# Part of the attention layer's input work placed among the expert layer's last picks, and table pieces placed in a down projection

## What is computed

```python
# expert layer: for each token 8 heads x 16 picks; u and v rows are gathered
act = gelu(einsum('pd,phkd->phk', xb, u_tab[idx]));  coef = gate * act
y = einsum('phk,phkd->pd', coef, v_tab[idx])
# attention layer: h = rmsnorm(x, norm1_g) * (1 + scale) + shift, for context and x
p = h @ w_in;  q = p[..., :1024];  k = rmsnorm(p[..., 1024:1280], kn_g);  v = p[..., 1280:1536]
q_l = apply_rope(rmsnorm(q_l, qn_g), cos, sin);  k_l = apply_rope(k_l, cos, sin)
# attends from x alone, to keys and values of context and x; then @ w_out
# feed-forward: h = x @ w_up (5632 wide); convolution over 3 tokens; (silu(g) * up) @ w_down
# S5: a diagonal complex recurrence; its powers come from tables of 32 x 256 complex numbers per row
```

## Time and profile before

| | us |
|---|---|
| median of 3 runs | 4437.26 (4435.03 to 4441.18) |
| the profiled execution | 4438.26 |
| its span, first to last instruction | 4436.5 |
| PE busy | 3674.1 (83%) |
| DVE busy | 2562.2 (58%) |
| peer_a's picks, first dot to last sum | about 1244 to 2589 |
| POOL's issue of one gather, 768 of them | median 0.946, at most 1.994 |
| Attention | about 2592 to 2741 |
| Ffn 0: first product, down projection, end | 3631, 3810, 3888 |

### The profile page before, as it was taken

How to read it: one execution, slowest core, us unless ns; L and a number is a source line. 1 busy time by engine, 2 the same in 40 slices (tenths; PEclk the granted TensorE clock), 3 DMA queues, 4 the chain that set the end, 5 groups by cost and what they waited for, 6 DMA issues and landing times.

```text
span 4436.5 us, 59216 instructions
## 1 busy us (share of the span) xinstructions
PE 3674.1 (83%) x22791; PEld 1989.2 (45%) x22791; DVE 2562.2 (58%) x5863; ACT 969.1 (22%) x2601; POOL 1257.3 (28%) x1273
## 2 busy tenths in 40 slices
PE   6898899888989987777777788887777889865999
PEld 2457744576444432222222235543222468432684
DVE  1345634556366777776777655667776349367341
ACT  0233312332132222222222213222222120010100
POOL 1005300242024444443444400344443000036000
PEclk7798899889999999999999999999999989976999
DMA  9410012000289999999999943999999324320443
GB/s 378 161 50 4 3 57 76 31 4 3 95 327 398 418 416 419 417 415 408 410 415 414 414 152 101 396 417 419 411 414 415 112 83 137 124 71 10 137 152 123
DMA packets 269478, 1043.49 MB, mean 235 GB/s; under 512 B 19394, under 2 KB 103596, under 8 KB 170896
## 3 DMA queue, kind: packets, MB, share of 16 engines
q0 software_dynamic: 114736, 815.52, 45.2%
q1 hardware_dynamic: 154464, 224.18, 15.0%
HBM read 1038.55 MB, written 1.08 MB: 234 GB/s over the span
## 4 chain that ended last, share of the span: by engine, by line
PE 49%; DMA 27%; DVE 13%; ACT 4%; POOL 4%; issue 4%; DVEq 0%; POOLq 0%; ACTq 0%
DMA arena<-in_peer_uv,arena 25%; PE psum L261 13%; PE psum L1748 10%; PE psum L299 4%; PE psum L742 4%; PE psum L1706 4%; PE psum L781 2%; DVE arena L1883 2%; DMA arena<-in_ada_w 2%; PE psum L212 2%; PE psum L1174 1%; POOL arena L2933 1%; POOL arena L1841 1%; PE psum L1083 1%; PE psum L1094 1%
## 5 line engine op out<-in xcount | busy, mean ns | idle before, releaser
L1748 PE MATMUL psum<-arena 128*128 128x512 f32 x3072 | 1454.9, 618 | 399.7 <-ACT arena L1783 393.8
L1883 DVE SCALAR_TENSOR_TENSOR arena<-arena 128x1024 bf16<-128x1024 f32 x768 | 940.9, 1225 | 526.2 <-DMA arena<-in_peer_uv,arena 493.4
L1841 POOL DMA_INDIRECT arena<-in_peer_uv,arena x768 | 863.4, 1124 | 1181.9 <-PE psum L1748 1036.5
L1748 PEld LDWEIGHTS psum<-arena 128*128 128x128 f32 x3072 | 571.9, 195 | 1234.2 <-ACT arena L1783 643.9
L261 PE MATMUL psum<-ring,arena 128*128 128x512 f32 (+2 forms) x1408 | 589.2, 581 | 25.5 <-DVE arena L2762 9.1
L261 PEld LDWEIGHTS psum<-ring,arena 128*128 128x128 f32 x1408 | 266.8, 197 | 342.1 <-issue 315.1
L1776 ACT ACTIVATE arena<-arena 128x2 f32<-128x2 f32 x384 | 78.2, 204 | 1248.7 <-DVE arena L1883 1248.7
L1783 ACT ACTIVATE arena<-consts,arena 128x128 f32<-128x128 f32 x768 | 268.4, 394 | 224.4 <-DVE arena L1895 220.9
L299 PE MATMUL psum<-arena,ring 128*128 128x256 f32 x1408 | 308.3, 380 | 9.2 <-DVE arena L2757 7.7
L299 PEld LDWEIGHTS psum<-arena,ring 128*128 128x128 f32 x1408 | 266.0, 190 | 49.5 <-issue 7.2
L742 PE MATMUL psum<-arena,ring 128*128 128x512 f32 x512 | 229.7, 603 | 1.6 <-issue 1.6
(11 more groups left out here) (401 smaller groups left out, 4000.7 us busy)
## 6 DMA issues: line engine op xcount, KB each, us to landing
arena<-in_ada_w SPq DMA_DIRECT2D x48, 1024.0 KB, 14.5
ring<-in_ffn_w_up SPq DMA_DIRECT2D x44, 1024.0 KB
ring<-in_dn_w_in SPq DMA_DIRECT2D x24, 1024.0 KB
ring<-in_peer_w_query SPq DMA_DIRECT2D x22, 1024.0 KB
ring<-in_ffn_w_down SPq DMA_DIRECT2D x20, 1024.0 KB
arena<-in_peer_uv,arena POOLq DMA_INDIRECT x768, 12.9
ring<-in_ev_w_in SPq DMA_DIRECT2D x10, 1024.0 KB
ring<-in_dn_w_out SPq DMA_DIRECT2D x8, 1024.0 KB
```

Source lines behind the costliest of these rows:

```text
L1748: m = e.matmul(k.banks[4 + t % 2 * 2 + nh], self.diag[g % self.ND], self.vsl[g % self.NS][:, nh * 512:(nh + 1) * 512], start=u % 8 == 0 an ...
L1841: e.indirect_dma_start(self.uv[g % self.NS], None, self.table(), bass.IndirectOffsetOnAxis(ap=self.eid[u % 6][:, s:s + 1], axis=0)).then_i ...
L1883: e.scalar_tensor_tensor(self.junk[g % 2], self.us[g % self.NS], 1.0, self.h[:, u // 8, :], MUL, MUL, accum_out=self.a[u % 2][:, s:s + 1]) ...
```

## The change

It has two parts.

**Norm, keys and values of attention.** A new class `EarlyRows` puts the norm of tiles 0 to 2 and their key and value projections into units 27 to 31 of peer_a, one step behind a pick s of unit u, with number i = 16 (u - 27) + s. ACT takes three squares (i = 0, 2, 4), one root with a table load (i = 8), six groups of four modulations (i = 22 to 40) and two pairs of copies (i = 52, 68). DVE takes a mean, a reciprocal and three scalings (i = 6, 11, 12, 14, 27). PE takes 8 transposes at each of i = 17, 21 and 33, and two products of 128x512 at i = 29 and then at every fourth step from 37 to 77. Attention keeps the norm of tile 3 and its 8 products; then come the queries. SP loads the key and value blocks ahead of the query blocks. DVE now works on the keys first and normalises the queries behind the last copy of the projection; the keys' transposes stand on PE ahead of the queries' ones.

**Table pieces.** In Ffn 0, DVE takes two pieces behind each convolution for c = 3 to 11 as before, and one from c = 12 on. What is left, 24 pieces, comes behind the last convolution, ahead of the additions of the down projection.

```diff
+    def early(self, u, s):
+        return 16 * (u - 27) + s if self.nt > 2 and u >= 27 else None
@@ Peer.pe_sum, and in the same way Peer.act and Peer.dve
+            if self.early(u, s) is not None:
+                k.early.pe(e, self.early(u, s))
@@ EarlyRows
+    def act(self, e, peer, i):
+        if i in (0, 2, 4):
+            e.activation(self.sq, st.k.X[:, t, :], ACT.Square, ..., accum_out=self.var[:, t:t + 1])
+        elif i == 8:
+            e.activation(self.var, self.var, ACT.Sqrt, bias=0.0, scale=1.0).then_inc(*S.up("n_sd"))
+        elif i in (22, 24, 26, 28, 38, 40):
...
+        elif i in (52, 68):
+            self.put(e, {52: 0, 68: 1}[i])
+    def pe(self, e, i):
+        if i in (17, 21, 33):
...
+        elif i >= 29 and i % 4 == 1:
+            n = 0 if i == 29 else (i - 33) // 4
+            if n < 12:
+                self.pe_kv(e, n // 4, n % 4 * 2, 2)
@@ Attention.sp
-        for p in (self.qp, self.kvp, self.op):
+        for p in (self.kvp, self.qp, self.op):
@@ Attention.pe
-        self.norm.pe(e)
-        for mark in self.norm.marks():
-            e.wait_ge(*mark)
+        e.wait_ge(*V.at("l_x"))
+        for half in range(2):
...
+        self.early.pe_kv(e, 3, 0, 8)
         self.qp.pe(e)
+        e.wait_ge(*S.at(("v", 3)))
+        for t in range(4):
+            self.kt[t].pe(e)
         e.wait_ge(*V.at(("q", 1, 512)))
-        self.kvp.pe(e)
-        e.wait_ge(*S.at(("v", 3)))
         self.qt.pe(e)
@@ Ffn
     def pieces(self, c):
-        return 0 if self.l or c < 3 else 2
+        return 0 if self.l or c < 3 else 2 if c < 12 else 1
@@ Ffn.dve
+        for _ in steps:
+            pass
         for n0 in (0, 512):
```

More of the change, by code:

```diff
@@ L1869, in dve @@
                     self.dve_coef(e, u, s // 2)
+                if self.early(u, s) is not None:
+                    k.early.dve(e, self.early(u, s))
             for _ in steps:
@@ L2060, in dve, with __init__, bank, put @@
                 e.tensor_scalar(dst, st.k.banks[4 + n % 4][:, 0:dst.shape[1]], self.sm[:, n:n + 1], None, MUL).then_inc(*V.up(("put", n)))
+class EarlyRows:
+    def __init__(self, st, kvp, A, B):
+        self.st, self.kvp, self.A, self.B = st, kvp, A, B
+        a = st.k.arena
+        self.sq, self.xn, self.var = a[:, 4096:5120], [a[:, 5120:6144], a[:, 6144:7168]], a[:, 12000:12003]
+    def bank(self, t):
+        return self.st.k.banks[(4, 5, 4, 5)[t]]
+    def act(self, e, peer, i):
+        st, P, V, S = self.st, self.st.P, self.st.V, self.st.S
+        if i in (0, 2, 4):
+            t = i // 2
+            e.wait_ge(*peer.V.at(("x", t)))
+            if t:
+                e.wait_ge(*S.at(("n_sq", t - 1)))
+            e.activation(self.sq, st.k.X[:, t, :], ACT.Square, bias=0.0, scale=1.0,
+                         accum_out=self.var[:, t:t + 1]).then_inc(*S.up(("n_sq", t)))
+        elif i == 8:
+            e.wait_ge(*V.at("n_mean"))
+            e.activation(self.var, self.var, ACT.Sqrt, bias=0.0, scale=1.0).then_inc(*S.up("n_sd"))
+        elif i in (22, 24, 26, 28, 38, 40):
+            t, half = {22: (0, 0), 24: (0, 1), 26: (1, 0), 28: (1, 1), 38: (2, 0), 40: (2, 1)}[i]
+            e.wait_ge(*P.at(("nt", t, half)))
+            for c in range(4 * half, 4 * half + 4):
+                e.activation(st.hT[:, c, t * 128:(t + 1) * 128], self.turned(t, half)[:, c % 4 * 128:(c % 4 + 1) * 128],
+                             ACT.Identity, scale=self.A[t][:, c:c + 1], bias=self.B[t][:, c:c + 1]).then_inc(*S.up(("nT", t, half)))
+        elif i in (52, 68):
+            self.put(e, {52: 0, 68: 1}[i])
+    def put(self, e, t):
+        st, S = self.st, self.st.S
+        e.wait_ge(*st.P.at(("kv", t)))
+        e.activation(st.kk[:, t, :], self.bank(t)[:, 0:256], ACT.Copy, bias=0.0, scale=1.0).then_inc(*S.up(("k", t)))
+        e.activation(st.v[:, t, :], self.bank(t)[:, 256:512], ACT.Copy, bias=0.0, scale=1.0).then_inc(*S.up(("v", t)))
+    def dve(self, e, i):
+        st, P, V, S = self.st, self.st.P, self.st.V, self.st.S
+        if i == 6:
+            e.wait_ge(*S.at(("n_sq", 2)))
+            e.tensor_scalar(self.var, self.var, 1.0 / 1024, 1e-06, MUL, ADD).then_inc(*V.up("n_mean"))
+        elif i == 11:
+            e.wait_ge(*S.at("n_sd"))
+            e.reciprocal(self.var, self.var).then_inc(*V.up("n_rs"))
+        elif i in (12, 14, 27):
+            t = {12: 0, 14: 1, 27: 2}[i]
+            e.wait_ge(*V.at("n_rs"))
+            if t == 2:
+                e.wait_ge(*P.at(("nt", 0, 1)))
+            e.tensor_scalar(self.xn[t % 2], st.k.X[:, t, :], self.var[:, t:t + 1], None, MUL).then_inc(*V.up(("n_x", t)))
+    def turned(self, t, half):
+        return self.st.k.banks[2 * t % 4 + half]
+    def pe(self, e, i):
+        st, P, V, S = self.st, self.st.P, self.st.V, self.st.S
+        if i in (17, 21, 33):
+            t = {17: 0, 21: 1, 33: 2}[i]
+            e.wait_ge(*V.at(("n_x", t)))
+            if t == 2:
+                e.wait_ge(*S.at(("nT", 0, 1)))
+            for half in range(2):
+                for c in range(4):
+                    m = st.turn(e, self.turned(t, half)[:, c * 128:(c + 1) * 128],
+                                self.xn[t % 2][:, (half * 4 + c) * 128:(half * 4 + c + 1) * 128])
+                m.then_inc(*P.up(("nt", t, half)))
+        elif i >= 29 and i % 4 == 1:
+            n = 0 if i == 29 else (i - 33) // 4
+            if n < 12:
+                self.pe_kv(e, n // 4, n % 4 * 2, 2)
+    def pe_kv(self, e, t, k0, nk):
+        st, P, V, S, ring = self.st, self.st.P, self.st.V, self.st.S, self.st.k.ring
+        if k0 == 0:
+            if t < 3:
+                e.wait_ge(*S.at(("nT", t, 1)))
+            if t == 2:
+                e.wait_ge(*S.at(("v", 0)))
+            if t == 3:
+                e.wait_ge(*S.at(("v", 1)))
+        for q in range(k0, k0 + nk):
+            key = (st.name, "kv", 0, q // 4 * 4)
+            if q % 4 == 0:
+                e.wait_ge(*ring.ready(key))
+            w = ring.buf(key).rearrange("p (k n) -> p k n", k=4)
+            m = e.matmul(self.bank(t), st.hT[:, q, t * 128:(t + 1) * 128], w[:, q % 4, :], start=q == 0, stop=q == 7)
+            if t == 3 and q == 3:
+                m.then_inc(*P.up())
+                ring.free(key, P)
+        if k0 + nk == 8:
+            m.then_inc(*P.up(("kv", t)))
+            if t == 3:
+                ring.free(key, P)
@@ L2069, in __init__ @@
         A, B = k.mod_cols(1, 0, range(4))
-        self.norm = Norm(self, range(4), self.hT, A, B, scr)
+        self.A, self.B, self.scr = A[3], B[3], scr
         self.q, self.kk, self.v = k.al2(2, 1024), k.al2(4, 256), k.al2(4, 256)
```

72 lines of the change are left out of this document (48 added, 24 removed).

## The result

| | before | changed |
|---|---|---|
| median of the runs, us | 4436.15 (4433.40 to 4441.18, 4 runs) | 4410.60 (4407.88 to 4411.86, 4 runs) |
| profiled execution, us (its span) | 4438.26 (4436.5) | 4411.86 (4410.1) |

The account below looks back on a forecast made before the run. Gathers were taken to bound the picks, a chain nearly all on PE attention, DVE Ffn 0's convolutions. 1.0 - 11.4 - 15.5 = -25.9 us from 4438.3 gave 4412.4, forecast as 4412 us, range 4403 to 4425.

Parts of the forecast that it names:

- What bounds the picks: Units 27 to 31 of peer_a: gathers at DMA share 1.01 are the bound, so work put there costs nothing if slots refill.
- The term of +1.0 us: Picks of units 27 to 31: the added work lengthens them by 1.0 us in sum.
- its 0.5 for the lumps: Picks: added work on PE, ACT and DVE, between nothing and the lumps at full length, taken as 0.5 us.
- its 0.45 for the two last products: End of unit 31: two products behind pick 13 are not covered and delay the last pair by 0.45 us.
- The port: Picks: DVE's three scalings might hold up POOL's gather issues, at worst 2.3 us in all; nothing was taken.
- Attention: From tile 3's addition to the first scores: 67.2 us in place of 78.6, 11.4 us less.
- the clock: Attention's eight key products: PE at its lower clock level costs 0 to 3.5 us; 1.0 was taken.
- Part 2: Ffn 0, c = 12 to 43: one piece per tile leaves PE the bound, 107.06 us for 122.55, 15.5 less.
- (a): Rival, units 27 to 31: ACT or PE delays are not caught up; 4424 us, to 4436; chance 0.14.
- (b): Rival, picks: slot loop without slack, every lump delays the gathers, 44 us in all; 4456 us; chance 0.04.
- (c): Rival, Ffn 0: something that remains holds PE or DVE, only half comes back; 4420 us; chance 0.12 together with (d).
- (d): Rival, attention: PE stays at its lower clock through the scores longer, rounds lose up to 5; 4417; 0.12 with (c).

Follow-up runs that it names:

- The second part alone: The kernel before with one table piece from c = 12 on and the rest in the down projection; median 4419.42 us, ratio 0.9950.
- the first alone: The changed kernel with two table pieces behind each convolution as before, norm, keys and values still among the picks; median 4430.24 us, ratio 0.9979.

## Why the prediction was right, step by step

- **What bounds the picks.** Right. The gathers run at 1.01 of the DMA engines with 6.7 us more of PE's work in the window, and the stretch from unit 27's first dot to the last pick product is as long as before. The term of +1.0 us was too large, by 1.1: of its 0.5 for the lumps nothing came that stands out of the scatter, and its 0.45 for the two last products shrank to 0.16 (6.07 us from the last dot to the last product for 5.91), since the last pair, which starts 5.25 us behind the one before it in place of 4.98, then takes 3.60 us without a gap ahead of it, and not 3.70.
- **The port.** The prediction took nothing for it, with up to 2.3 us at worst. Nothing is what came, -0.1 us over 80 picks with three scalings of 0.75 us on DVE among the gathers. The Trainium skill's page "SBUF — State Buffer", section "Who interferes with whom", has POOL's descriptors wait for such a scaling. The trace agrees for two of the three, each of which held one issue of a gather (the rows under the experiments), for 0.15 and 0.28 us; the third met none. The 1.93 us of the earlier trace rows were not a scaling's doing but a dot's, which ran from 2339.23 to 2340.45. The dots do this to some 200 issues in each trace, with the gathers at 1.0 of the DMA engines, so the slots hid such waits long before the scalings came.
- **Attention.** 67.9 us for 67.2, 10.7 less than before and not 11.4. Its terms, from the chain above: norm of tile 3 7.28 (7.2 forecast), key products 8.97 to the start of the queries' (6.9 + 1.0), queries 27.67 (27.7), copies 2.05 (2.4), queries' norm 19.17 (19.2), transposes and the last copy 2.75 (2.8). The step that was mis-sized is the clock: it cost 2.0 us, inside the 0 to 3.5 given, where 1.0 was taken. The bound itself was added up wrongly: seven products of 0.87 us at half speed would cost 6.1 us more, not 3.5. The kernel with added products showed that it is the clock (7.10 us at 1.00); over the other executions without such products the eight took 8.61 to 10.07 us, so the cost is 1.5 to 3.0 us, and 2.0 is one draw of it. The rest is the copies', 0.35 less.
- **Part 2.** 107.05 us for 107.06 forecast. The late pieces had 6.4 us of cover left, 10 forecast: they took 30.0 us for 29, and the first sum came 2.3 us earlier. The 2.3 us at the down projection's start were missing from the sum: the earlier trace rows gave the 38.72 us that DVE waits there, but I did not ask at what clock PE starts behind the gap that the late convolutions leave. The second part alone has all of this gain (38.47 us), the first alone 0.6 of it (40.18 for 40.75); why the first has any stays open.
- **The sum.** -0.1 - 10.7 - 15.5 - 2.3 = -28.6 against -25.9 worked out; 1.1 of the difference is the picks, 2.3 the clock of the down projection, less 0.7 in attention. The profiled execution came to 26.4 less only because the unchanged stretches add 2.2. So the nearness of 4410.6 to 4412 is in part luck: the terms were short of the gain by 2.7 us, and scatter of nearly that size stood against it.
- **The rivals.** (a) falls by the picks' stretch, (b) by the executions with more lumps on ACT and PE. The windows' free time on PE, 10 us per 41, was the right measure for (b)'s point of decision, and the reading that three engines' lumps add up was not: with 44 products more, where PE alone is over, the changed kernel's gain is gone. (c) falls, the pace is PE's throughout. (d), a cold array for longer at the scores, falls: the rounds and the output took 70.27 us as before. There was something to be had there all the same, 1.45 us, since before they had begun cold too.

## What to carry to other kernels

Where a stretch is bound by transfers with several buffers ahead, work for the other engines is free there up to the idle time of the fullest engine, summed over the stretch and not lump by lump (shown here for PE, with lumps of 1.7 to 3.5 us, and for ACT with lumps of 2.8 us, where the limit was not reached); add it up for the engine that gets the most, since beyond it every us counts. Where work is moved out of a chain, look for what it covered: here 19 us of a norm on DVE stood bare behind it, and splitting it, so that half runs beside the projection, brought 7.8 us more. And where an edit shortens a wait of TensorE, read the granted clock behind that wait, in the kernel before: what starts cold there is a term of its own.

## What the runs showed of the hardware that was not expected

- After an idle gap of 6.96 us the down projection began at 0.50 to 0.51, and 16 products took 15.69 us in place of 13.97 (first part alone). After one of 2.18 us the changed kernel began it at 1.00. All ten executions with the second part and the parameters in their old place took 38.46 or 38.47 us to the first addition. The two kernels that make the tables' parameters earlier, more than 100 us ahead of this place, have the same 2.18 us, and both took 40.16 us; in the one shown above 0.60 and 15.67 us followed. In both PE was busy without a break at 1.00 in the 12 us before (windows of 4 us, 4.00 busy in each). Why the clock fell in these two stays open.
- A load of an activation table took 1.28 us and the root behind it followed at once (0.02 us); eight of them, with most of the loads back, cost the picks nothing beyond their scatter of half a us.
- Of the 768 issues of a gather on POOL in the changed kernel 214 began while a dot on DVE had more than 0.14 us to run. 210 of these lasted until 0.81 to 0.83 us behind the dot's end, so 0.97 to 2.00 us; the other four began within 0.04 us of the dot's start and took 0.94. The 354 issues that were running when a dot began took 0.94 to 0.96 us: which of the two came first decides. Of 34 that began during a `tensor_reduce` none took over 0.95 us.
- The same eight products behind the same gap of 6.78 us and the same transposes took 8.6 to 10.1 us from one execution to another (7.10 to 7.11 in all three with added products).
- Stretches that no edit touched differ by up to 9 us from one execution to another (1244.3 to 1253.2 us to the first dot), more than most terms of this sum, while others repeat within 0.02 us (107.05 for 31 tiles in every kernel with the second part).
